# A hybrid decoder step: forget rows written during the projections, GpSimd kept out of the attention stage, convolution steps dealt out between the halves of attention items

## The reference

```python
def ab_project(h, w_in, b_f, q_g, k_g):
    proj = h @ w_in
    a_in, q, k, v, fg = jnp.split(proj, [...], axis=-1)
    q = rms_norm(q.reshape(*lead, H_B, HEAD_DIM), q_g)
    k = rms_norm(k.reshape(*lead, H_B, HEAD_DIM), k_g)
    logf = jax.nn.log_sigmoid(fg.astype(jnp.float32) + b_f.astype(jnp.float32))
    return a_in, q, k, v, logf

def conformer_conv(a_in, hist, conv_w, conv_b, ln_g, ln_b):
    val, gate = jnp.split(a_in, 2, axis=-1)
    full = jnp.concatenate([hist, val * jax.nn.sigmoid(gate)], axis=1)
    out = <depthwise causal convolution of full with 31 taps> + conv_b
    return jax.nn.silu(layer_norm(out, ln_g, ln_b)), full[:, -(CONV_WIDTH - 1):]

def fox_attend(q, k, v, f_q, f_k, q_pos, k_pos):
    s = jnp.einsum('nqhd,nkhd->nhqk', q, k).astype(jnp.float32) * ATTN_SCALE
    s = s + <f_q by row> - <f_k by column>        # f: running sums of logf
    p = jax.nn.softmax(jnp.where(mask, s, -jnp.inf), axis=-1)
    return jnp.einsum('nhqk,nkhd->nqhd', p.astype(v.dtype), v)
```

## Time and profile before

| | |
|---|---|
| median of 3 runs | 1289.99 us (1288.89 to 1292.57) |
| the profiled execution's own time | 1292.44 us |
| its span in the profile | 1290.6 us |
| PE busy | 1249.4 us, 97% of the span |
| DVE, ACT, POOL busy | 621.8, 465.7, 99.1 us |

### The profile page before, as it was taken

One profiled execution on the slowest core, in us unless ns is written; L12 is line 12 of the kernel. 1 busy time (PEld: TensorE's weight loads), 2 busy tenths in 40 slices (PEclk: granted clock), 3 DMA queues, 4 the chain that ended last, 5 costly groups with the idle time before them and its releaser, 6 DMA issues.

```text
span 1290.6 us, 23160 instructions
## 1 busy us (share of the span) xinstructions
PE 1249.4 (97%) x9778; PEld 1208.2 (94%) x9778; DVE 621.8 (48%) x875; ACT 465.7 (36%) x785; POOL 99.1 (8%) x132
## 2 busy tenths in 40 slices
PE   6999998889999999999999999989999999999998
PEld 5999985659999999999999999989999999999998
DVE  5798887554543343343344435654533433433431
ACT  5636645633441231232233424534421322322321
POOL 3010300001200000000001231042000000000000
PEclk9999997979999999999999999999999999999999
DMA  5331320342332322322322222112322322322322
GB/s 155 101 112 38 97 87 35 115 132 66 99 101 96 99 77 88 98 82 81 98 90 75 73 100 90 66 60 76 99 85 80 99 91 73 98 97 66 99 66 70
DMA packets 111756, 113.16 MB, mean 88 GB/s; under 512 B 6430, under 2 KB 105898, under 8 KB 111663
## 3 DMA queue, kind: packets, MB, share of 16 engines
q1 hardware_dynamic: 110111, 107.50, 26.0%
q0 software_dynamic: 1472, 4.41, 1.1%
q10 hardware_dynamic: 88, 0.02, 0.0%
HBM read 107.18 MB, written 5.16 MB: 87 GB/s over the span
## 4 chain that ended last, share of the span: by engine, by line
PE 90%; DVE 4%; ACT 3%; DMA 1%; issue 1%; POOL 1%; SPq 0%; ACTq 0%; DVEq 0%
PE ps L672 78%; PE ps L911 5%; PE ps L824 1%; DMA w_raw<-in_w_in_ab 1%; PE ps L854 1%; DVE c_f L1597 1%; PE ps L871 1%; PE ps L836 1%; POOL A_lo L647 1%; DVE a_f L1942 1%; DVE w_lo L1514 0%; PE ps L972 0%; PE ps L797 0%; PE ps L946 0%; DVE prob L1688 0%
## 5 line engine op out<-in xcount | busy, mean ns | idle before, releaser
L672 PE MATMUL ps<-A_hi,w_hi 128*128 128x272 f32 x1408 | 293.7, 290 | 8.5 <-DVE xT L1540 4.3
L672 PE MATMUL ps<-A_lo,w_hi 128*128 128x272 f32 x1408 | 292.1, 289 | 0.0
L672 PE MATMUL ps<-A_hi,w_lo 128*128 128x272 f32 x1408 | 291.2, 288 | 0.0
L1156 ACT ACTIVATE w_hi<-w_raw 128x1024 fp32r<-128x1024 f32 x180 | 189.3, 1052 | 265.2 <-DVE xT L1839 249.2
L672 PE MATMUL ps<-B_hi,w_hi 128*128 128x272 f32 x1280 | 266.0, 289 | 0.0
L672 PE MATMUL ps<-B_lo,w_hi 128*128 128x272 f32 x1280 | 265.0, 288 | 0.0
L672 PE MATMUL ps<-B_hi,w_lo 128*128 128x272 f32 x1280 | 263.8, 288 | 0.0
L672 PEld LDWEIGHTS ps<-A_hi,w_hi 128*128 128x128 f32 x1408 | 222.0, 189 | 10.1 <-ACT xT L1186 4.7
L1514 DVE TENSOR_TENSOR w_lo<-w_raw,w_hi 128x1024 fp32r<-128x1024 f32 x180 | 219.8, 1221 | 5.2 <-ACT w_hi L1156 5.1
L672 PEld LDWEIGHTS ps<-A_hi,w_lo 128*128 128x128 f32 x1408 | 222.2, 189 | 0.0
L672 PEld LDWEIGHTS ps<-A_lo,w_hi 128*128 128x128 f32 x1408 | 220.6, 189 | 0.0
(11 more groups left out here) (272 smaller groups left out, 1013.1 us busy)
## 6 DMA issues: line engine op xcount, KB each, us to landing
w_raw<-in_w_ff_up SPq DMA_DIRECT2D x64, 512.0 KB, 4.3
w_raw<-in_w_ff_down SPq DMA_DIRECT2D x64, 512.0 KB, 4.3
w_raw<-in_w_in_ab SPq DMA_DIRECT2D x20, 512.0 KB, 4.7
w_raw<-in_w_in_c SPq DMA_DIRECT2D x16, 512.0 KB, 4.3
w_raw<-in_w_out_ab SPq DMA_DIRECT2D x8, 512.0 KB, 4.7
k_pg<-in_cache_k SPq DMA_DIRECT2D x16, 256.0 KB, 4.4
v_pg<-in_cache_v SPq DMA_DIRECT2D x16, 256.0 KB, 3.7
w_raw<-in_w_out_c SPq DMA_DIRECT2D x8, 512.0 KB, 4.0
```

The costliest lines, as they stand in the source:

```text
L672: mm = pe.matmul(ps[:, 2 * s + half, 0:HALF], wt[:, j % 4, k, :], mv[:, k, half * HALF:(half + 1) * HALF], start=(k == 0 and at_ == 0), st ...
L1156: act.activation(w_hi[:, j % 4], w_raw[:, b % 2, :, P * (j % 2):P * (j % 2) + P], ACT.Copy)\
```

## The change

It has five parts.

- `forget_rows` goes from after item 10 into projection iteration 13, and its two tiles move to memory of their own.
- GpSimd no longer stores the values and no longer clears `q_bd`. SP starts the two stores, ahead of the gathers of the value pages; ACT clears `q_bd` in item 11 by an activation of 128 x 1024.
- In the projections DVE's iteration m is put in another order: half of its convolution steps, `head_factor(m-1)`, `w_lo`, sampled taps, the other half, and `sums(m)` last, where `sums(m)` stood first (behind `key_gain`).
- In an item, steps stand between `maximum` and `share` (the larger half) and after `share`. `CONV_NAT` adds up to 91 steps for 85, and of the seven iterations with items the four with a single item get one step more (the rounding adds none to the others), so that one step is left for the items that stand alone, where eleven were left before.
- SP loads key pages 3 and 4 before value page 3, not after it.

```diff
-CONV_NAT = (3, 2, 4, 0, 4, 0, 3, 3, 2, 4,
-            3, 2, 0, 2, 3, 0, 2, 3, 2, 3,
-            4, 3, 3, 3, 5, 4, 5, 4, 5, 4)
+CONV_NAT = (3, 2, 4, 1, 4, 1, 3, 4, 2, 4,
+            4, 2, 1, 2, 4, 1, 2, 3, 2, 4,
+            4, 3, 3, 2, 5, 3, 6, 3, 6, 3)
...
                     sp.wait_ge(prep_done, 1)
+                    sp.wait_ge(v_evac, 2 * TT)
+                    sp.dma_start(o["v_prompt"][0, 0].rearrange("(t p) h d -> p t (h d)", p=P), v_nat[:, 1:TT, :]).then_inc(v_stored, 16)
+                    sp.dma_start(o["v_sample"][0].rearrange("b q h d -> (b q) (h d)"), v_nat[0:NS, 0, :]).then_inc(v_stored, 16)
                     for j in range(4):
+                        if j == 3:
+                            keys(3)
+                            keys(4)
                         sp.wait_ge(s_done, QT * (2 * j + 2))
                         gather(i["cache_v"], v_pg[j], j, vpg_in[j])
-                    for b2 in range(3, NB):
+                    for b2 in range(5, NB):
                         keys(b2)
...
-            pool.wait_ge(v_evac, 2 * TT)
-            store(o["v_prompt"][0, 0].rearrange("(t p) h d -> p t (h d)", p=P), v_nat[:, 1:TT, :])
-            store(o["v_sample"][0].rearrange("b q h d -> (b q) (h d)"), v_nat[0:NS, 0, :])
-
-            pool.wait_ge(nat_done, 6 * TT)
-            pool.memset(q_bd[:, :, :, :], 0.0).then_inc(bd_zero, 1)
...
+            def clear_queries():
+
+                act.wait_ge(nat_done, 6 * TT)
+                link(act.activation(q_bd[:, :, :, :].rearrange("p a b c -> p (a b c)").rearrange("p (a c) -> p a c", c=P),
+                                    ones[:, :].rearrange("p (a c) -> p a c", a=1).broadcast_to([P, PAIRS * NB * HQ // P, P]),
+                                    ACT.Copy, scale=0.0))
...
                 item_slot(s)
+                if s == 11:
+                    clear_queries()
                 if 12 <= s < 12 + H:
-                    if s == 12:
-                        act.wait_ge(bd_zero, 1)
                     sample_prep(s - 12)
...
-            def item_slot(s):
+            def item_slot(s, steps):
                 if s <= FIRST_ALONE:
                     maximum(s + 2)
+                    conv(steps - steps // 2)
                     share(s + 1)
...
                 else:
                     if s + 3 < H * QT:
                         maximum(s + 3)
+                    conv(steps - steps // 2)
                     if s + 2 < H * QT:
                         share(s + 2)
+                conv(steps // 2)
                 if s % (2 * QT) == 1 and s > 2 * QT:
                     pair_lo(s // (2 * QT) - 1)
...
             for m in range(6 * TT):
+                items = ITEMS.get(m - 4 * TT, ())
                 if 2 * TT <= m - 2 < 4 * TT:
                     key_gain(m - 2)
-                if m < 4 * TT:
-                    sums(m)
+                if not items:
+                    conv(CONV_NAT[m] // 2)
                 if 1 <= m < 4 * TT + 1:
                     head_factor(m - 1)
...
-                for s in ITEMS.get(m - 4 * TT, ()):
-                    item_slot(s)
                 if TT < m < 5 * TT and m % TT in (1, 3):
                     n = N_NAT + 2 * (m // TT - 1) + m % TT // 2 + 4
                     split_lo(n, n)
                 if m in SAMPLED_AT:
                     sampled_taps(SAMPLED_AT[m])
-                conv(CONV_NAT[m])
+                if m == 13:
+                    forget_rows()
...
+                for s in items:
+                    item_slot(s, (CONV_NAT[m] + (s == items[0])) // len(items))
+                if not items:
+                    conv(CONV_NAT[m] - CONV_NAT[m] // 2)
+                if m < 4 * TT:
+                    sums(m)
 
             for s in range(FIRST_ALONE, H * QT):
-                item_slot(s)
-                if s == FIRST_ALONE:
-                    forget_rows()
-                conv(CONV_ATT)
+                item_slot(s, CONV_ATT)
```

More of the change, by code:

```diff
@@ L172, in build @@
         f_aug = sb("f_aug", [P, 2, TT * H, 2], F32)
-        e_nat = sb("e_nat", [P, TT], F32)
         n_small = sb("n_small", [P, 6, 4], F32)
@@ L203, in build @@
         junk = at("junk", [P, D], F32, zone_t)
+        e_nat = at("e_nat", [P, TT], F32, zone_t + 8192)
         nat_sq = at("nat_sq", [P, 2, 256], F32, zone_t + 2048)
@@ L229, in build @@
         kn_T = at("kn_T", [P, PAIRS, NS], F32, reg1 + 4096)
-        nf_T = at("nf_T", [H * NB, KS], F32, reg1 + 4608)
-        self_q = at("self_q", [H * NB, 2, P], F32, reg1 + 5760)
-        assert 6784 <= CT * TB
         kc_T = [at(f"kc_T{s}", [P, PAIRS, NEWC], F32, reg2 + 4096 * s) for s in range(4)]
@@ L246, in build @@
         glu_nat = at("glu_nat", [NS, 2, DA], F32, zone_pt)
+        nf_T = at("nf_T", [H * NB, KS], F32, zone_pt + 6656)
+        self_q = at("self_q", [H * NB, 2, P], F32, zone_pt + 6656 + 4 * KS)
+        assert zone_pt + 6656 + 4 * KS + 8 * P <= nc.sbuf_usable_end and 4608 <= CT * TB
         pt_sb = at("pt_sb", [1, NB * PAGES], I32, zone_pt + 8192 - 64 - 1536)
@@ L311, in build @@
         x_in = [sem(f"x_in{g}") for g in range(4)]
-        xs_in, xc_done, psum_red, bd_zero, prep_done, silu_done = (sem("xs_in"), sem("xc_done"), sem("psum_red"),
-                                                                   sem("bd_zero"), sem("prep_done"), sem("silu_done"))
+        xs_in, xc_done, psum_red, prep_done, silu_done = (sem("xs_in"), sem("xc_done"), sem("psum_red"),
+                                                                   sem("prep_done"), sem("silu_done"))
         act_seq, dve_seq, pool_seq = sem("act_seq"), sem("dve_seq"), sem("pool_seq")
@@ L338, in build @@
         g_done, vn_T, vn_ok, mix_done, mix_ok = sem("g_done"), sem("vn_T"), sem("vn_ok"), sem("mix_done"), sem("mix_ok")
-        yT_done, y_ok, stored = sem("yT_done"), sem("y_ok"), sem("stored")
+        yT_done, y_ok, stored, v_stored = sem("yT_done"), sem("y_ok"), sem("stored"), sem("v_stored")
         vm_done, vx_done, vs_done, vv_done, vr_done, vy_done = (sem("vm_done"), sem("vx_done"), sem("vs_done"),
@@ L486, in _ @@
             sp.wait_ge(stored, 6 * 16)
+            sp.wait_ge(v_stored, 2 * 16)
         @block.gpsimd
@@ L1698, in forget_rows @@
                 dve.wait_ge(fs_done, 1)
-                dve.wait_ge(nat_done, 6 * TT)
                 dve.tensor_scalar(nf_T[:, :], ps[0:NB * H, 6, 0:KS], -1.0, None, ALU.mult)
@@ L1742, in _ @@
                     split_lo(11, 11)
-                if m == 4 * TT + 2:
-                    maximum(0)
-                    maximum(1)
-                    share(0)
-                for s in ITEMS.get(m - 4 * TT, ()):
-                    item_slot(s)
                 if TT < m < 5 * TT and m % TT in (1, 3):
@@ L1753, in _ @@
                     sampled_taps(SAMPLED_AT[m])
-                conv(CONV_NAT[m])
+                if m == 13:
+                    forget_rows()
+                if m == 4 * TT + 2:
+                    maximum(0)
+                    maximum(1)
+                    share(0)
+                for s in items:
[4 more added lines that the diff above has]
+                    sums(m)
             for s in range(FIRST_ALONE, H * QT):
-                item_slot(s)
-                if s == FIRST_ALONE:
-                    forget_rows()
-                conv(CONV_ATT)
+                item_slot(s, CONV_ATT)
                 if s in (LN_MEAN + 2, LN_MEAN + 3):
```

## The result

| | before | changed |
|---|---|---|
| median | 1289.24 us (8 runs, 1288.46 to 1292.57) | 1295.08 us (8 runs, 1293.37 to 1298.51) |
| ratio, 95% interval | | 1.0041, 1.0027 to 1.0056 |
| the profiled execution: own time, span | 1292.44, 1290.6 | 1298.51, 1296.5 |
| its mean granted clock | 0.988 | 0.987 |

The change makes the kernel slower by 0.41%. It was forecast at 1293.5 us, inside 1282 to 1298. Measured from its own before the loss is 5.8 us (1295.08 - 1289.24), where the forecast had 3.5.

What follows compares the result with a forecast made beforehand. PE was busy 97% of the span, so only its waits or lower clock could matter. Projections +4.5, double items +2.3, after tile 29 -2.3 and lost steps -1.0 gave +3.5 us: 1293.5 us, range 1282 to 1298.

Steps and rivals of the forecast that it cites:

- The projections: Head transposes wait on a loop through DVE's late `sums(m)` and ACT's copy: +4.5 us by iteration 21, bounds -2.8 and +6.
- the holds of iterations 4, 6 and 7: PE's waits in the projections for `qT` and `kT` behind the late sums: 1.0, 0.7 and 2.3 us.
- the 0.4 of iteration 9: A further PE delay of 0.4 us in projection iteration 9, counted in the 3.8 us late at m = 10.
- the fourth rival: Projections: the 2.3 us hold in iteration 7 lowers the clock there too; +3, about 1296.5 us; chance 0.15.
- The double items: Two items behind one tile (m = 24, 26, 28): `turn_probs` waits 0.9, 0.6, 0.8 us more for `share`; +2.3 us.
- After tile 29: Chain from `maximum(11)` to `scores(14)` takes 5.3 us instead of 7.6, with PE idle 0.4, 0.9 and 1.6 us: -2.3 us.
- The clock: After tile 29 the clock falls as before, and the 15 us at half speed stay.
- the second rival: The clock stays up after tile 29: 7.5 to 9.5 us less than the forecast, about 1285.0 us; chance 0.22.
- The size taken for the rest, -1.0: Once the clock is up again, DVE no longer has a step in each item: -1.0 us, bounds 0 and -2.5.
- the piece of 1.22 us: A single idle piece of PE at 244.7 us in the kernel before, read as bringing no clock fall.
- the prediction's own 0.3%: What a measurement of this kernel can tell: about 0.3%, 3.9 us.
- "same": The outcome inside that 3.9 us, given 0.41, against faster 0.27 and slower 0.32.

Runs made afterwards that it cites:

- steps behind: The changed kernel with an iteration's convolution steps put behind its items, the sums still last: 1289.39 us, ratio 1.0011.
- old projections: The changed kernel with sum, inverse, `w_lo`, taps and all steps in the old order where there are no items: 1293.10 us, ratio 1.0039.
- with both: The changed kernel with DVE's old order in the projections and the steps behind the items' maxima and shares: 1289.26 us, ratio 1.0001.

## Why the prediction was right, and where it was not

**The projections: +4.5 forecast, 4.5 to 5.7 measured.** Followed tile by tile, DVE came out within 0.4 us (`sums(3)` ends at 99.96 for 100.3, `w_lo` starts at 109.94 for 110.3, `sums(6)` ends at 112.82 for 113.1), the holds of iterations 4, 6 and 7 at 1.01, 0.63 and 2.27 for 1.0, 0.7 and 2.3; the 0.4 of iteration 9 did not come. Where the clock did not fall the stage is 4.5 us longer than before (72.44 and 72.42 for 67.92): 3.8 us by iteration 10 and 0.8 from there to 21, for 3.8 and 0.7 forecast. In the profiled execution it is 5.7, because the fourth rival came true in it as well: the hold of 2.3 us brought half speed from about 115.5 to 119 us, 1.2 us against the execution without it (the rival had 3). That the late sum is enough to cause it is shown by the kernel before with that line alone. That it is the only cause, as the working implied by naming the sum alone, is wrong. The steps ahead of the inverse cost 4.4 us without it (73.99 for 69.63). The two together cost 2.8 (72.4 for 69.6), less than either alone; I put that down to both standing in the same round, which is not shown. The other 1.7 of the 4.5 are the forget rows in iteration 13 and the fuller table.

**The double items: +2.3 forecast, +2.6 measured**, of which 2.1 are waits of 0.80, 0.60 and 0.71 us (forecast 0.9, 0.6, 0.8); they went when the steps were put behind.

**After tile 29: -2.3 forecast, -0.9 measured.** From the first `scores` behind tile 29 to `scores(14)` it takes 7.39 us (206.98 to 214.37), for 8.33 before. The idle pieces were forecast at 0.4, 0.9 and 1.6 and are 0.41, 0.93 and 1.70. The step that failed in size is the one that took `values(4)` and `scores(13)` behind them at their full-speed 0.4 and 0.8 us: the clock was already down at 211, and they took 0.69 and 1.65. The chain on DVE, from `maximum(11)` at 207.68 to `values(4)` at 212.20, took 4.5 us for 4.1.

**The clock.** It fell after tile 29 as forecast, for 13.7 us (about 15 forecast), and the second rival did not come. That such a fall follows the waits is likely but not shown: fewer and shorter waits went with a higher mean clock, but the same pieces brought it in one run and not in another. The size taken for the rest, -1.0, came close partly by luck: from `scores(14)` to the pages it takes 45.42 us, for 46.55 before. The stretch at half speed behind `scores(14)` was 4.7 us shorter (10.3 for 15.0), by an estimate worth about 2.3 us at PE's full load, where the forecast had it the same. A fall that was not forecast took 1.6 us back: the products at 252.07 us (L871) took 5.58 us, for 3.94 before. The prediction had read the piece of 1.22 us ahead of them as one that brings no fall. That leaves about -0.4 for DVE's lost steps, in place of the -1.0.

**The sum.** The forecast's +3.5 became +6.2 by the stages and +5.8 by the medians. By the stages the difference is 1.2 in the projections (the fall of the clock), 0.3 in the value tiles and 1.2 from tile 29 to the pages (-2.1 for -3.3). The median lies between the forecast and its fourth rival (1293.5 and 1296.5). By the prediction's own 0.3% the change is slower, at 0.41%, where "same" was held likeliest.

**What the parts are worth, one by one:** forget rows early -0.15%, in spite of 0.8 us more in the projections; GpSimd's work moved, nothing that the median shows, and 1.3 us of PE's idle time in one profile; the sum last alone 5.6 us of the projections, the steps ahead of the inverse alone 4.4, both together 2.8; the steps inside items 2.6 us of the value tiles, and by the ratios 0.30 to 0.47% with the new projections (1.0041 or 1.0058 to 1.0011) and 0.38% with the old; the fuller table with the forget rows in iteration 13, 1.6 us (69.61 to 68.01 when both were taken back). The key pages' order was not tried alone; no wait in any of the lists is for a page's transfer.

By the ratios alone the order in the projections shows little: put back, it takes 1.0011 to 1.0001 with the steps behind the items, and 1.0041 or 1.0058 to 1.0039 with the steps inside. The granted clock differs between these groups. An estimate that takes it out is each execution's time multiplied by its mean granted clock, which is right as far as PE has work while the clock is down. It averages 1281.7 and 1281.2 us for the changed kernel, 1279.4 with the old projections, 1279.1 with the steps behind, 1275.4 with both, and 1275.9 to 1276.7 for the kernel before. By it the order in the projections is worth 1.8 to 3.7 us, for 2.8 by the stage.

## What to carry to other kernels

In a round that goes through several in-order engines, filling work belongs behind the last instruction of the round that another engine waits for; here two instructions of 0.16 to 0.41 us, each moved behind a step or two, cost 2.8 us of the stage, and putting back one of them gave nothing. Before a wait is taken away, look for what else ends within the same microsecond: behind the blocked `share` stood two roundings on another engine, and the last move of these alone took the ratio from 0.9984 to 0.9954. And set one profile against another by stages and with their granted clocks beside them, since executions of one program differ by more than such a change is worth.
